# Router products in groups of four with constants loaded in the output stage, residual and gate rows all turned ahead of the token table

## The reference, cut to what matters

```python
def _layer(x, c, l, hist, p):
    mod = (silu(c) @ p['w_ada'][l] + p['b_ada'][l]).reshape(B, 6, D_MODEL)
    sh1, sc1, g1, sh2, sc2, g2 = ...
    h = _rmsnorm(x, p['norm_g'][l, 0]) * (1 + sc1) + sh1
    mix, st = _token_mixers(h, l, hist, p)      # input projection z, mLSTM, sparse attention, pooling, w_out
    x = x + g1 * mix
    h = _rmsnorm(x, p['norm_g'][l, 1]) * (1 + sc2) + sh2
    ffn = _swiglu(...) if l % 2 == 0 else _moe(...)
    return x + g2 * ffn, st

def _moe(h, w_router, b_router, we1, we3, we2):  # layer 1 only
    logits = x @ w_router + b_router             # 8 experts
    top_v, top_i = lax.top_k(logits, 2)
    gates = softmax(top_v)
    y = sum over e of comb[:, e:e+1] * _swiglu(x, we1[e], we3[e], we2[e])
```

## Time and profile before

| what | value |
|---|---|
| median of three runs | 2183.32 us |
| profiled execution, its own time | 2189.17 us |
| its span in the profile | 2187.5 us |
| granted TensorE clock, mean of the span | 0.953 |
| PE busy | 2027.0 us (93%) |
| stage route and what leads to it (1443 to 1484 us) | 41 us, PE busy 26.3 |
| start of ffn (1484 to 1502 us) | 18 us, PE busy 14.2 |

### The profile page before, as it was taken

One profiled execution on the slowest core, in us unless ns is written; L12 is line 12 of the kernel. 1 busy time (PEld: TensorE's weight loads), 2 busy tenths in 40 slices (PEclk: granted clock), 3 DMA queues, 4 the chain that ended last, 5 costly groups with the idle time before them and its releaser, 6 DMA issues.

```text
span 2187.5 us, 36988 instructions
## 1 busy us (share of the span) xinstructions
PE 2027.0 (93%) x14437; PEld 1709.7 (78%) x14437; DVE 1287.7 (59%) x2036; ACT 1016.2 (46%) x1528; POOL 180.5 (8%) x271
## 2 busy tenths in 40 slices
PE   6999978898999999998999788988899999999996
PEld 4999845588999999998999545866666667788883
DVE  2657643355544544456666643556565667789885
ACT  5522235543433433335222455435445566677782
POOL 3000120110000000000000021111010010010102
PEclk7999878998999999999999889989999999999998
DMA  9221588532645364552122366217677789899995
GB/s 329 72 78 58 157 227 293 181 130 74 174 127 165 119 173 140 159 152 81 60 77 85 72 234 203 89 52 272 217 267 238 256 281 337 333 370 370 375 384 189
DMA packets 272096, 418.25 MB, mean 191 GB/s; under 512 B 21214, under 2 KB 216312, under 8 KB 271952
## 3 DMA queue, kind: packets, MB, share of 16 engines
q1 hardware_dynamic: 249984, 349.50, 48.5%
q0 software_dynamic: 21968, 66.72, 9.5%
HBM read 385.73 MB, written 29.59 MB: 190 GB/s over the span
## 4 chain that ended last, share of the span: by engine, by line
PE 82%; DMA 5%; DVE 5%; ACT 4%; issue 2%; ACTq 0%; DVEq 0%; POOL 0%; PEldq 0%; SPq 0%; PEld 0%; POOLq 0%
PE banks L951 78%; PE banks L955 4%; DMA expert_ring<-in_we 3%; DMA weight_ring<-in_w_ada 1%; ACT scratch L1911 1%; DVE scratch L2566 1%; DVE region L2566 1%; DVE weights_lower L2566 0%; DMA scratch<-bias_rows 0%; ACT region L1911 0%; ACT region_split L1911 0%; ACTq L1926 0%; ACT hidden_t L1911 0%; ACT mix_t L1911 0%; DVEq L2559 0%
## 5 line engine op out<-in xcount | busy, mean ns | idle before, releaser
L951 PE MATMUL banks<-upper_parts,region_split 128*128 128x320 f32 x1664 | 391.3, 311 | 4.5 <-DVE upper_parts L2566 4.5
L951 PE MATMUL banks<-upper_parts,weights_lower 128*128 128x320 f32 (+1 forms) x1248 | 387.3, 310 | 0.0
L951 PE MATMUL banks<-region_split 128*128 128x320 f32 (+1 forms) x1264 | 339.5, 332 | 3.8 <-DVE upper_parts L2566 3.8
L2566 DVE TENSOR_TENSOR expert_lower<-expert_ring,region_split 128x1408 fp32r<-128x1408 f32 (+1 forms) x198 | 284.2, 1468 | 88.6 <-PE banks L951 64.5
L951 PEld LDWEIGHTS banks<-upper_parts,region_split 128*128 128x128 f32 x1664 | 285.5, 189 | 4.8 <-issue 4.8
L1911 ACT ACTIVATE region_split<-expert_ring 128x1408 fp32r<-128x1408 f32 (+1 forms) x198 | 242.5, 1256 | 59.3 <-DMA expert_ring<-in_we 58.9
L951 PEld LDWEIGHTS banks<-region_split 128*128 128x128 f32 x1264 | 223.4, 188 | 20.1 <-issue 4.3
L951 PEld LDWEIGHTS banks<-upper_parts,weights_lower 128*128 128x128 f32 (+1 forms) x1248 | 235.6, 189 | 0.0
L951 PE MATMUL banks<-region_split,upper_parts 128*128 128x384 f32 x732 | 226.8, 380 | 0.0
L2566 DVE TENSOR_TENSOR weights_lower<-weight_ring,region_split 128x2048 fp32r<-128x2048 f32 (+2 forms) x72 | 168.9, 2350 | 96.6 <-ACT region_split L1911 96.5
L1911 ACT ACTIVATE region_split<-weight_ring 128x2048 fp32r<-128x2048 f32 (+2 forms) x72 | 140.6, 1959 | 164.4 <-PE banks L951 162.8
(11 more groups left out here) (336 smaller groups left out, 3241.4 us busy)
## 6 DMA issues: line engine op xcount, KB each, us to landing
expert_ring<-in_we SPq DMA_DIRECT2D x176, 704.0 KB, 7.1
expert_ring<-in_we SPq DMA_DIRECT2D x121, 512.0 KB, 4.5
weight_ring<-in_w_ada SPq DMA_DIRECT2D x48, 1024.0 KB, 8.8
weight_ring<-in_w SPq DMA_DIRECT2D x88, 512.0 KB, 4.7
weight_ring<-in_w_in SPq DMA_DIRECT2D x24, 1024.0 KB, 5.2
weight_ring<-in_w SPq DMA_DIRECT2D x16, 1408.0 KB, 6.2
weight_ring<-in_w_out SPq DMA_DIRECT2D x8, 1024.0 KB, 6.2
y_rows<-residual_t POOLq DMA_DIRECT2D x4, 1760.0 KB, 24.8
```

Of the source, the lines that this page charges most:

```text
L951: return nc.tensor.matmul(out, lhsT, rhs, start=first, stop=last)
L2566: return v.tensor_tensor(out, x, y, op)
```

## The change

- Layer 1's router constants are loaded when DVE has cleared the router's place (`router_place_cleared`, in the out stage) in place of after the out stage; SNUM and PFIRST move in the scratch so that this is free of overlap.
- PE waits for the hidden blocks of the router products four at a time (two waits in place of eight).
- PE gets filler products: 8 ahead of the z products of both layers, 6 ahead of the router products, 3 between their two groups, 8 ahead of the mask sums, 2 ahead of the token table's products.
- All ten half tiles of the residual and all four of the gates are turned in the route stage, ahead of the token table; ACT copies all 14 and spreads the gates (DVE did three plus two and the spreading). Nothing of this is left at the start of ffn.
- FIRST_ROWS goes from 6 to 4.

```diff
-FIRST_ROWS = 6
+FIRST_ROWS = 4
...
-        EARLY_ROWS = [(t, half) for t in range(NT) for half in range(2)][:5]
-        LATE_ROWS = [(t, half) for t in range(NT) for half in range(2)][5:] + [("gates", i, half) for i in range(2) for half in range(2)]
-        KEPT_BY = ["dve", "dve", "act", "act", "act", "act", "dve", "dve", "dve"]
+        EARLY_ROWS = [(t, half) for t in range(NT) for half in range(2)] + [("gates", i, half) for i in range(2) for half in range(2)]
...
                 if l % 2:
-                    after(f"out{l}")
+                    pool.wait_ge(router_place_cleared, 1)
                     load(router_in,
...
                 claim(0, 1, 2, 3)
+                fill(0, 8)
                 for k in range(KD):
                     take(z_hidden_split)
...
                     take(router_in, 112)
-                    claim(0, 1)
+                    claim(0, 1, 2)
+                    fill(2, 6)
                     for k in range(KD):
-                        wait(modulated, 4 * KD + k + 1)
+                        if k % 4 == 0:
+                            wait(modulated, 4 * KD + k + 4)
                         at = slice(32 * (k % 4), 32 * (k % 4 + 1))
                         mm(PS[at, 0, :], WRT[:, k, :], HT[:, k, 0:TP], k < 4, k >= 4)
+                        if k == 3:
+                            fill(2, 3)
...
+                    claim(3)
+                    fill(3, 8)
                     take(masks_ready)
-                    claim(3)
...
-                    for u, (t, half) in enumerate(EARLY_ROWS):
+                    for u, unit in enumerate(EARLY_ROWS):
                         b = 4 + (2 * NT + u) % 4
                         claim(b)
+                        if unit == ("gates", 1, 0):
+                            wait(gates_spread, 1)
                         for j in range(4):
-                            ins = tr(PS[:, b, tiles(j)], XT[:, 4 * half + j, tiles(t)])
+                            k = 4 * unit[-1] + j
+                            if unit[0] == "gates":
+                                columns = GATES_SPREAD[:, k, :] if unit[1] else MOD[:, l, 5 * KD + k, 0:1].broadcast_to([P, P])
+                                ins = mm(PS[:, b, tiles(j)], columns, ident[:, :], True, True)
+                            else:
+                                ins = tr(PS[:, b, tiles(j)], XT[:, k, tiles(unit[0])])
                         hand(ins, "act", b)
                     claim(0, 1)
+                    fill(0, 2)
...
-                    for u, unit in enumerate(LATE_ROWS):
...
                     for u, unit in enumerate(EARLY_ROWS):
+                        if u == 2 * NT:
+                            copy(GATES_SPREAD.rearrange("p k (b t) -> p k b t", t=TS), along(MOD[:, l, 5 * KD:6 * KD, 1:], 3, TS)).then_inc(gates_spread, 1)
                         take(for_act)
                         drained(copy(kept_rows(unit), PS[:, 4 + (2 * NT + u) % 4, :].rearrange("p (k c) -> p k c", c=P)))
```

More of the change, by code:

```diff
@@ L388, in build @@
         BRB, WRT, BEFORE, PNUM, TOKF = g(NE), g(KD, 32), g(P), g(MOST_PASSES + 1, parts=1), g(NT)
+        SNUM, PFIRST = g(PASS), g(MAX_PASSES + 1)
         MS, MSUM = g(NT * NE // 2).bitcast(BF16), g((NT + 1) * NE // 2).bitcast(BF16)
@@ L392, in build @@
         S1F, S2F = S12[:, 0, :], S12[:, 1, :]
-        LOGT, SNUM, PFIRST, REST = g(T), g(PASS), g(MAX_PASSES + 1), g(2, NT)
+        LOGT, REST = g(T), g(2, NT)
         REACHED, IN_PASS = g(2, NT, MAX_PASSES + 1), g(2, NT, MAX_PASSES)
@@ L490, in build @@
         h_rows_ready, h_rows_out = sem("h_rows_ready"), sem("h_rows_out")
+        router_place_cleared = sem("router_place_cleared")
         logits_out, one_hots_ready, table_ready = sem("logits_out"), sem("one_hots_ready"), sem("table_ready")
@@ L2420, in _ @@
                         upper(FE)
[L2421 to L2424, removed]
                     for half in range(2):
@@ L3031, in _ @@
                 if l % 2:
-                    v.memset(WRT[:, :, :], 0.0)
+                    v.memset(WRT[:, :, :], 0.0).then_inc(router_place_cleared, 1)
                 lower(0)
@@ L3277, in down @@
                                 copy(YB_RIDERS, PS[:, 2, 0:D // 4]).then_inc(rider_y_ready, 1)
[L3279 to L3287, removed]
                     for half in range(2):
```

## The result

Measured: 2195.84 us in the median of 20 runs, beside 2187.2 us of the kernel before in 20 runs on the same chip; ratio 1.0032, 95% interval 1.002 to 1.0044. The change costs 7.0 us (4.4 to 9.6) where I had forecast a gain of 2.8. It is under the 0.5% that I had set as the bound, but it has the other sign, and the time lies 8 us above my range. A smaller part of the miss is the base: the three runs shown at first had their median 3.9 us under that of the twenty.

The account below looks back on a forecast made before the run. PE was taken to bound the expert passes (busy 496.4 of 500 us), the order of small steps the stretch from 1443 to 1484 us. Terms -1.0 - 1.8 + 0 + 0 = -2.8 us, from 2183.3 to 2180.5 us; range 2174 to 2188.

Parts of the forecast that it names:

- Router constants earlier, waits in groups of four: Router products: the last blocks set the time, so both gain 0; bounds 0 to -0.3 us and 0 to +3.7 us.
- the second rival: Router group: the single wait leaves PE idle, low clock until logits are summed; price 3.7 us, 2184.2 us, chance 0.13.
- All rows ahead of the token table: Route stage: fillers keep the clock up, one-hot products run at full clock, the token table comes 1.4 us earlier.
- FIRST_ROWS 4 and nothing late in ffn: Start of ffn: gather lands 3.2 us earlier, PE starts cold, first expert products 1.8 us earlier, the table's 1.4 included.
- Fillers at z: Start of the z stages: clock up earlier gains 1.0 us in layer 1, capped by DVE; 0 in layer 0.
- The third: Route stage: early rows at low clock delay the table 3.2 us, gather issued later; 2184.6 us, slower, chance 0.17.
- the first rival: Gather in ffn: transfer shared with weight rows as before, PE cold, start of products unchanged; 2182.3 us, chance 0.20.

Follow-up runs that it names:

- b_const: The kernel before with early router constants, one wait for four blocks and the nine fillers there; ratio 1.0014 to the kernel before.
- a_keep: The changed kernel without z fillers, plus 12 fillers behind the one-hot products and 28 ahead of turning the gathered rows; 2188.35 us, ratio 1.0014.
- a_late: The changed kernel with the nine late units back in ffn, without the ten fillers ahead of mask sums and table; 2191.08 us, ratio 1.0023.
- a_z1: The changed kernel with the z fillers in layer 1 only; ratio 1.0052 to the kernel before.
- b_z1: The kernel before with the eight z fillers in layer 1 only; ratio 1.0018 to the kernel before.
- a_warm: The changed kernel with 36 fillers where the late rows stood, ahead of turning the gathered rows; 2196.05 us, ratio 1.0051, six runs.

## Why the prediction was wrong, step by step

**Router constants earlier, waits in groups of four: 0.** Right within the error of the times (+0.7, error 1.0), and by luck in the profiled execution: the clock dropped to 0.50 between 1460 and 1463, as the second rival feared, but only the first group ran in it; the second and all behind it were at 1.00, and from the `ones` products to the one-hot products it was 37.5 us, 37.3 before. In the seven other kernels with such groups the second group ran at the low clock too and the one-hot products began 1 to 2 us later (5 in one), as said under b_const.

**All rows ahead of the token table: -1.4 for the table.** The size was wrong, -0.25. The clock held (1.00 from 1464 to 1490), ACT's pace was as forecast (4.98 us for ten units), its last unit ended at 1481.5 on before's scale, in time. But the one-hot products took 2.52 us at the full clock, where I had under 2; I had put their length down to the low clock (2.93), and it hardly depends on it. And PE came to them 0.2 us later than before.

**FIRST_ROWS 4 and nothing late in ffn: -1.8.** This is the first step that failed, and its sign: from the one-hot products to the first expert product it took 3.0 us more, and the times give the early rows +4.6 us (0.9). The account had two errors. The landing came 0.7 us earlier in place of 3.2: 0.25 from the table in place of 1.4, the rest from the two rows in place of 1.8; in the mean of five traces they give 1.5. And the price of a cold PE was counted as 1.4 us (turns 0.6, riders 0.8) with the rides at the full clock. Measured, everything up to the first expert product ran cold: turns +0.9, riders +1.65, rides +1.4 in the profiled execution and +1.7 to +1.9 in the four others with the rows early and nothing in the wait. I had taken from the earlier trace rows that the clock is up again after 3.5 us of work; here it took 9, from 1498.54 until past 1507. In the kernel before those 3.5 us stood 2.39 us behind the one-hot products, here behind 10.51 us of idle. The late rows that I removed were not only 9 us of work in a wait: the clock rose while they ran, ahead of the path. a_keep's trace shows it (3.4 us), and so do the stretches of the 15 kernels named there; the times agree (a_late against a_z1 -6.0, error 1.9; a_keep -3.7, error 1.7). Late rows don't make the rides safe: in a_late and b_z1, which have them, the clock fell again in the rides (5.75 and 5.68 us).

**Fillers at z: -1.0 in layer 1, 0 in layer 0.** This is the second step that failed, with +3.8 us (0.7) in the times. Layer 1's was nearly right where I looked, 0.75 us: the clock stands at 1.00 at the first blocks, and the wait for DVE's third block, now 1.12 us, caps the gain,

```profile
1011.00:1012.00 1.00, 1.00 (x9) 1.00 (x8) 1.00 (x3) 0.84 (x2) 0.00 (x0) 1.00 0.00 0
...
1015.58 0.39 PE L950 MATMUL banks<-upper_parts,z_weights_upper 128*100 128x320 f32 x1 [1.12 <-DVE hidden_lower_parts L2564]
```

where in the earlier trace rows the clock still had its mean of 0.53 four us behind the start of the blocks. For layer 0 no cost is seen (a_z1). What I missed stands 190 us later: +4.3 us in the memory stage, in the mean of eight traces against six. "PE is the bound behind it" was taken to mean that a gain comes through to the end; it holds up to the next stage whose length hangs on the clock, and no further.

**Rivals.** The second, router cold, held in most kernels with such groups, at 1 to 2 us and not 3.7. The third had the right sign and the right place of cause (all rows in front), but another mechanism: ACT's pace held and the table wasn't late. The Trainium skill's page "DMA: Bandwidth & Descriptors", section "Queues, rings and completion order", from which I drew the first rival, has the queues taking turns; by it two rows fewer help only once the rows in front are through. The traces, with 1.5 us for them, are near my 1.8 and speak against that rival. The range was too narrow since each case had its bound in the stage that it touched.

## What to carry to other kernels

Before you move work out of a wait, ask what it does for the clock of the work behind the wait: at 1.2 GHz turns, riders and rides cost 4 us more here, and a wait filled with 40 useless products let the expert products begin 3.4 us sooner than an idle one. Count the gain of a stage only if the next stages don't depend on when they start; where PE works in pieces with gaps, take traces of several versions and compare the length of the same stretch before believing a microsecond. With executions spread over 8 to 22 us, a part is judged from several kernels that have it and several that haven't.

## What was not expected of the hardware

One and the same instruction stream took between 93.5 and 104.0 us in one stretch, with clock means of 0.84 to 0.70, in kernels that differ by small shifts ahead of it or not at all; a delay of 1.4 us cost 5.1 (1.5) in all. The clock fell within 2.4 us of idle behind 23 us at the full level (a_warm), and in the same trace again in the rides, with PE idle for only 0.57 us ahead of them.
